# Input projection: a fifth column group in split precision, its low parts on GpSimd, and the S5 phase products on VectorE

## What is computed

```
h = rmsnorm(x) * w
a_v, a_g, b_u, c_z, c_xbc, c_dt = split(h @ w_in)      # w_in 2048 x 4112
ya = conformer_conv(a_v, a_g)                          # 31 taps, layernorm, silu
yb = s5(b_u)                                           # complex diagonal recurrence, 32 groups x 64 states
yc = mamba2(c_z, c_xbc, c_dt)                          # 4 taps, state-space product
x  = x + concat(ya, yb, yc) @ w_out
x  = x + cross_attention(rmsnorm(x), mem_k, mem_v)     # mem_k, mem_v = rmsnorm(mem) @ wk, @ wv
x  = x + conv_ffn(rmsnorm(x))
```

## Time and profile before

| | us |
|---|---|
| median of 3 runs | 1803.45 (1802.83 to 1803.63) |
| the profiled execution | 1805.04 |
| its span | 1803.3 |
| busy: TensorE, VectorE, ScalarE, GpSimd | 1784.9, 1139.3, 739.2, 258.9 |

### The profile page before, as it was taken

The page is one execution under the profiler, slowest core; times in us unless marked ns, Lnnn a source line. Parts: engine busy times, 40 slices in busy tenths (PEclk is TensorE's granted clock), DMA queues, the critical chain, the costliest instruction groups (busy, mean ns, idle before and its releaser), DMA issues.

```text
span 1803.3 us, 32857 instructions
## 1 busy us (share of the span) xinstructions
PE 1784.9 (99%) x12594; PEld 1640.2 (91%) x12594; DVE 1139.3 (63%) x1976; ACT 739.2 (41%) x1111; POOL 258.9 (14%) x273
## 2 busy tenths in 40 slices
PE   8999999999999999999999999999999999999998
PEld 7877898777779999866999999999999999999998
DVE  6999888888775564443456556665655566546444
ACT  3100575444453343342245344444433345444444
POOL 1024200133421310000132000000000000003200
PEclk9999999999999999999999999999999999999999
DMA  8333544556667585487555555555555556554552
GB/s 255 106 117 106 198 140 138 176 182 208 196 209 240 164 303 164 153 327 265 154 164 164 164 163 163 163 163 164 164 166 165 165 148 185 166 163 160 167 163 99
DMA packets 158390, 316.49 MB, mean 176 GB/s; under 512 B 16986, under 2 KB 39531, under 8 KB 153492
## 3 DMA queue, kind: packets, MB, share of 16 engines
q1 hardware_dynamic: 153525, 307.73, 54.5%
q10 hardware_dynamic: 4776, 7.56, 1.4%
HBM read 300.78 MB, written 14.89 MB: 175 GB/s over the span
## 4 chain that ended last, share of the span: by engine, by line
PE 93%; DVE 4%; DMA 2%; ACT 1%; issue 0%; ACTq 0%; SPq 0%; DVEq 0%
PE bank L909 22%; PE bank L911 21%; PE bank L910 21%; PE bank L872 20%; PE bank L1467 2%; PE bank L1479 1%; DVE xc L2638 1%; DMA kv<-in_cache_mem_v 1%; DMA xtok<-in_x_prompt 1%; PE bank L1489 1%; PE bank L1278 0%; DMA raw<-in_w_out 0%; DVE raw_lo L2665 0%; PE bank L1097 0%; PE bank L958 0%; PE bank L1312 0%
## 5 line engine op out<-in xcount | busy, mean ns | idle before, releaser
L909 PE MATMUL bank<-hhi,whi 128*128 128x288 f32 x2128 | 631.9, 297 | 0.9 <-DVE wlo L2918 0.9
L910 PE MATMUL bank<-hlo,whi 128*128 128x288 f32 x2128 | 628.5, 295 | 0.0
L911 PE MATMUL bank<-hhi,wlo 128*128 128x288 f32 x2128 | 626.3, 294 | 0.0
L2918 DVE TENSOR_TENSOR wlo<-raw,whi 128x1024 fp32r<-128x1024 f32 (+1 forms) x270 | 329.7, 1222 | 377.7 <-ACT whi L1950 377.1
L1950 ACT ACTIVATE whi<-raw 128x1024 fp32r<-128x1024 f32 (+1 forms) x270 | 283.2, 1049 | 509.8 <-PE bank L911 501.9
L911 PEld LDWEIGHTS bank<-hhi,wlo 128*128 128x128 f32 x2128 | 401.6, 189 | 0.0
L909 PEld LDWEIGHTS bank<-hhi,whi 128*128 128x128 f32 x2128 | 399.3, 188 | 2.3 <-DVE wlo L2918 1.9
L910 PEld LDWEIGHTS bank<-hlo,whi 128*128 128x128 f32 x2128 | 400.2, 188 | 0.1
L872 PE MATMUL bank<-hT,raw 128*128 128x288 f32 x640 | 160.1, 409 | 0.0
L872 PEld LDWEIGHTS bank<-hT,raw 128*128 128x128 f32 x640 | 120.0, 190 | 35.0 <-issue 3.1
L1877 ACT ACTIVATE khi<-raw 128x1024 fp32r<-128x1024 f32 x66 | 69.9, 1059 | 109.5 <-PE bank L872 106.4
(11 more groups left out here) (551 smaller groups left out, 2744.4 us busy)
## 6 DMA issues: line engine op xcount, KB each, us to landing
raw<-in_ffn_w_down SPq DMA_DIRECT2D x86, 512.0 KB, 3.8
raw<-in_ffn_w_gate SPq DMA_DIRECT2D x80, 512.0 KB, 3.7
raw<-in_ffn_w_up SPq DMA_DIRECT2D x80, 512.0 KB, 3.7
raw<-in_w_in SPq DMA_DIRECT2D x64, 512.0 KB, 3.7
raw<-in_xa_wk SPq DMA_DIRECT2D x32, 512.0 KB, 3.9
raw<-in_xa_wv SPq DMA_DIRECT2D x32, 512.0 KB, 4.2
raw<-in_w_out SPq DMA_DIRECT2D x32, 512.0 KB, 3.8
raw<-in_xa_wq SPq DMA_DIRECT2D x32, 512.0 KB, 4.0
```

What stands on the lines that cost most here:

```text
L909: pe.matmul(out, lhsT=wh[:, wo:wo + P], rhs=xh, start=first, stop=False)
L910: pe.matmul(out, lhsT=wh[:, wo:wo + P], rhs=xl, start=False, stop=False)
L911: return pe.matmul(out, lhsT=wl[:, wo:wo + P], rhs=xh, start=False, stop=last)
L2918: tt(wlo[:, s % 2, wsl], raw[:, s % 4, wsl], whi[:, s % 2, wsl].bitcast(F32), ALU.subtract)\
```

## The change

Five things change together:

- Slabs 32 to 39, the fifth group, become split slabs (`SPLIT_AT` 40 to 32).
- The low parts of slabs 32 to 47 are made by GpSimd (L783 of the changed kernel, semaphore `in_lo_g`), those of slabs 48 to 63 still by VectorE (`LOW_V`). The buffers stay as they were.
- The phase products go from GpSimd to VectorE: those of iteration j-1 stand between the turn of j and its adds. The turn back of j-1 goes ahead of the scans of j.
- TensorE feeds pairs 6 and 7 after slabs 33 and 36 (32 and 34 before), and takes the outputs of pairs 5, 6 and 7 after slabs 36, 39 and 42 (35, 37 and 39 before).
- ScalarE's list follows: `x_high` and the high parts of slabs 32 to 34 come ahead of the conformer's first taps, those of 35 to 41 before the loop over slabs 40 to 63. Four small additions of the conformer's input (`glu_a`) move from iterations 10 to 13 to iterations 6 to 9, and the last S5 output (`s5_y(3)`) from slab 41 to slab 43.

```diff
-        S5_IN = (17, 20, 22, 25, 27, 30, 32, 34)
+        S5_IN = (17, 20, 22, 25, 27, 30, 33, 36)
...
-        SPLIT_AT = 40
+        SPLIT_AT, LOW_V = 32, 48
+        S5_OUT = (22, 25, 27, 30, 32, 36, 39, 42)
...
-            for j in range(SJ):
-                pool.wait_ge(*at("s5_scanned", j + 1))
-                g_ = gri[:, j % 2, :, :]
-                if j >= 1:
-                    pool.wait_ge(*at("s5_h", 2 * j))
-                pool.tensor_tensor(hAB[:, 0, :, :], g_, tabC[:, j, :].unsqueeze(1).to_broadcast([P, 2, NP]),
-                                   ALU.mult).then_inc(S("s5_prod"), 1)
-                pool.tensor_tensor(hAB[:, 1, :, :], g_, tabS[:, j, :].unsqueeze(1).to_broadcast([P, 2, NP]),
-                                   ALU.mult).then_inc(S("s5_prod"), 1)
...
+            for x in range(SPLIT_AT, LOW_V):
+                pool.wait_ge(*at("kw_hi", x - SPLIT_AT + 1))
+                pool.tensor_tensor(raw_lo[:, x % 4, :], raw[:, x % 4, :], ihi_slot(x).bitcast(F32), ALU.subtract)\
+                    .then_inc(S("in_lo_g"), 1)
...
-                    if split:
-                        pe.wait_ge(*at("kw_lo", sl - SPLIT_AT + 1))
+                    if split and sl < LOW_V:
+                        pe.wait_ge(*at("in_lo_g", sl - SPLIT_AT + 1))
+                    if sl >= LOW_V:
+                        pe.wait_ge(*at("kw_lo", sl - LOW_V + 1))
...
-                    if x == S5_IN[pair] + 5:
+                    if x == S5_OUT[pair]:
                         s5_out(pair)
...
+            x_high(range(12))
+            in_split(32)
+            x_high(range(12, 14))
+            in_evac(3)
+            in_split(33)
+            x_high(range(14, KT))
+            in_split(34)
...
+            def s5_products(j):
+
+                v.wait_ge(*at("s5_scanned", j + 1))
+                g_ = gri[:, j % 2, :, :]
+                if j >= 1:
+                    v.wait_ge(*at("s5_h", 2 * j))
+                for i, tab in enumerate((tabC, tabS)):
+                    tt(hAB[:, i, :, :], g_, tab[:, j, :].unsqueeze(1).to_broadcast([P, 2, NP]), ALU.mult)\
+                        .then_inc(S("s5_prod"), 1)
...
+                if j >= 1:
+                    s5_products(j - 1)
...
-                me.sync()
+                gri_done = me.n
+                if j >= 1:
+                    s5_turn_back(j - 1)
+                me.reach(gri_done)
```

More of the change, by code:

```diff
@@ L65 @@
     "dve_norms": (("hmix", 16), ("hxa", 16), ("hffn", 16)),
-    "pool_setup": (("bsel", 2), ("s5_prod", 2 * SJ), ("s5_fin", 2), ("conf_sum", 2)),
+    "pool_setup": (("bsel", 2), ("s5_fin", 2), ("in_lo_g", 16), ("conf_sum", 2)),
     "pe_mixers": (("glu_mm", 4), ("ex_mm", 5), ("mem_t", 8), ("ps_t", 1),
@@ L1208, in kv_group @@
                     sl = NA + 8 * g + s
-                    pe.wait_ge(*at("kw_lo", N_SPLIT + 8 * g + s + 1))
+                    pe.wait_ge(*at("kw_lo", N_LOW_V + 8 * g + s + 1))
                     wh = khi[:, sl % 2, :].rearrange("p (k n) -> p k n", k=2)
@@ L1767, in _, with x_high, in_split @@
             in_evac(2)
+            def x_high(tiles):
+                for k in tiles:
+                    wait_used_A(sc_, 24 + k // 2)
+                    sc_.wait_ge(*at("x_lo", k + 1))
+                    a(xhi[:, k, :], hT[:, k, :], ACT.Copy).then_inc(S("x_hi"), 1)
+            def in_split(x):
+                wait_raw(sc_, x // 4, x % 4)
+                if x >= SPLIT_AT + 2:
+                    wait_used_A(sc_, x - 2)
+                if x == 48:
+                    sc_.wait_ge(*at("s5_prod", 2 * SJ))
+                    sc_.wait_ge(*at("s5_turned", 2 * SJ))
+                a(ihi_slot(x), raw[:, x % 4, :], ACT.Copy).then_inc(S("kw_hi"), 1)
+            x_high(range(12))
+            in_split(32)
+            x_high(range(12, 14))
             in_evac(3)
+            in_split(33)
+            x_high(range(14, KT))
+            in_split(34)
             def first_tap(dst, dst_s, src, src_s, w, b, name):
@@ L1790, in gelu @@
                     a(uT[:, t, :], uT[:, t, :], ACT.Gelu_apprx_tanh).then_inc(S("s5_gelu"), 1)
[L1792 to L1807, removed]
             def mem_square(t):
@@ L1815, in mem_square @@
                   accum_out=msum[:, t:t + 1]).then_inc(S("mem_sq"), 1)
-            x_high(range(12))
-            in_split(SPLIT_AT)
-            x_high(range(12, 14))
+            for x in range(35, 41):
+                in_split(x)
             in_evac(4)
-            in_split(SPLIT_AT + 1)
-            x_high(range(14, KT))
+            in_split(41)
             def mem_rows(t, c0, c1):
@@ L1877, in k_split @@
                 a(khi[:, y % 2, :], raw[:, y % 4, :], ACT.Copy).then_inc(S("kw_hi" if y < NKV else "w_hi"), 1)
-            for x in range(SPLIT_AT, NA):
+            for x in range(40, NA):
                 if x == NA - 1:
@@ L1882, in _ @@
                     k_split(0)
-                elif x > SPLIT_AT:
+                elif x > 40:
                     in_split(x + 1)
@@ L2543, in last_state, with in_split @@
                     me.step(v.tensor_copy(fin[:, i, j:j + 1], hri[:, j % 2, i, NP - 1:NP]))
+            def in_split(x):
+                v.wait_ge(*at("kw_hi", x - SPLIT_AT + 1))
+                tt(raw_lo[:, x % 4, :], raw[:, x % 4, :], ihi_slot(x).bitcast(F32), ALU.subtract)\
+                    .then_inc(S("kw_lo"), 1)
             for j in range(SJ):
@@ L2563, in _ @@
                     .then_inc(S("s5_scanned"), 1)
-                if j in (10, 11, 12, 13):
-                    glu_a((j - 10,))
+                if j in (6, 7, 8, 9):
+                    glu_a((j - 6,))
                 if 2 <= j < 10:
                     x_low((6 + j,))
-                if j >= 1:
-                    s5_turn_back(j - 1)
                 if j == 8:
@@ L2573, in _ @@
                     s5_y(1)
+            s5_products(SJ - 1)
             s5_turn_back(SJ - 1)
@@ L2644, in conv_c @@
                         q.then_inc(S("conv_c_taps"), 1)
-            def in_split(x):
-                v.wait_ge(*at("kw_hi", x - SPLIT_AT + 1))
-                tt(raw_lo[:, x % 4, :], raw[:, x % 4, :], ihi_slot(x).bitcast(F32), ALU.subtract)\
-                    .then_inc(S("kw_lo"), 1)
-            in_split(SPLIT_AT)
-            in_split(SPLIT_AT + 1)
             def mem_lo(k):
@@ L2672, in _ @@
                        60: (14, 16), 61: (17, 17)}
-            for x in range(SPLIT_AT, NA):
+            for x in range(40, NA):
                 if x == NA - 1:
                     k_split(0)
-                elif x > SPLIT_AT:
+                elif x >= LOW_V - 1:
                     in_split(x + 1)
@@ L2679, in _ @@
                     s5_y(2)
+                if x == 43:
                     s5_y(3)
```

1 line of the change is left out of this document (added).

## The result

The changed kernel takes 1823.31 us at the median of four runs (1822.35 to 1824.58) against 1803.54 for the kernel before: 1.0103 of it, 95% interval 1.0090 to 1.0116. It is 19.8 us slower. (The ratios here and in the table are those on record. They are not the quotients of the two medians, from which they differ by some 0.002 at most; here that quotient is 1.0110.) I had forecast slower, 1811.5, and a range that ended at 1819. The profiled execution took 1822.77 us, its span is 1821.1, 17.8 longer than before's.

The account below looks back on a forecast made before the run. TensorE, busy 99% of the span, was taken to bound the kernel. Profiled 1805.0 plus 8.0 (slab 43 +6.2, slabs 44 to 47 +1.5 and +0.3) gave 1813.0, less 1.6 for the median: 1811.5 us; range 1799 to 1819.

Parts of the forecast that it names:

- step 5: SyncE's queue: glu_w and raw slab 43 wait for the last product; slab 43 starts 11.5 us after it, +6.2.
- step 6: Slabs 44 to 47: turns through ScalarE and GpSimd of 3.56 us against 3.19, +1.5, and lengthening by taps, +0.3.
- Step 4: Recurrence: each GpSimd low part of 2.2 us costs VectorE 1.65; last product at about 213, 8.5 us later.
- rival C: Recurrence: scans held too or GpSimd starved, 2.35 us per part; last product at 220, 1818.5 us; chance 0.20 with D.
- rival D: Products on VectorE are dear, waiting for GpSimd's parts; shows as long L2540; C's time, 1818.5; chance 0.20 with C.
- Step 1: Slabs 32 to 39 become split on TensorE, 3.19 instead of 3.88 us each, saving 5.5 us while fed.
- Step 2: Recurrence's earliest end by TensorE's feeding: last product at 203.8 us, now about 204.5, so nothing gained or lost.
- Step 3: VectorE's recurrence loop: moving products there costs nothing, a 1.08 us stall exchanged for 1.2 of work; iteration 5.2 us.
- The check on VectorE's side: Loop 8.5 later, five low parts add 8.2, eight parts removed give -9.1: +7.6 us, about TensorE's +8.0.
- Rival A: Recurrence: low parts hide in turns, scans and waits; last product at 203.8, slab 43 earlier, 1798 to 1800.5 us; chance 0.17.
- From slab 48 on nothing differs: From slab 48 to the end, the accumulated lateness stays unchanged.

Follow-up runs that it names:

- e7: Changed kernel with each low part on GpSimd replaced by two memsets of the same tile, correction left out; 1803.20 us, 0.9996 of the kernel before.
- e5: Changed kernel with 24 unused matmuls on TensorE filling the stop ahead of slab 43; 1820.27 us, 1.0112 of the kernel before.
- e11: Changed kernel with GpSimd's low parts replaced by two memsets and SyncE's product wait and glu_w load behind raw slab 44; 1799.67 us, 0.9967 of the kernel before.
- e3: Kernel before with only the phase products moved to VectorE and the turn back ahead of the scans; 1805.69 us, 1.0006 of the kernel before.
- e6: Changed kernel with every GpSimd low part cut to its first 512 columns, used for both slab halves; 1803.83 us, 1.0000 of the kernel before.
- e4: Kernel before with only the low parts of slabs 40 to 47 moved to GpSimd; 1808.96 us, 1.0022 of the kernel before.
- e1: Changed kernel with SyncE's last-product wait, glu_w load and two mtok loads moved behind raw slabs 46 and 47; 1819.61 us, 1.0070 of the kernel before.

## Why the prediction was wrong

The direction held, and so did the chain of causes: low parts hold VectorE, the last product is late, SyncE's queue passes it on, slab 43 stops. The sizes failed in two steps: the last product came 7.0 us later than forecast, step 5 took 0.6 less, and step 6 took 3.4 more. That is 9.8, the whole of 17.8 less 8.0.

**Step 4, the price of a part, was the one that failed.** I put it at three quarters of 2.2, 1.65 us, and took off 2.5 for parts that fall into waits: last product at 213. Measured: 1.97 a part, 19.7 for ten; with 199.0 that is 218.7, and it came at 220.0. I left it open whether a scan is held, and priced a part from a row that had only an add beside it; the rows of after and e7 show that scans are held while GpSimd reads, and not while it only writes. A part was also longer than 2.2 us, 2.35 at least. And the 2.5 had nothing to be taken from: a loop that is late has no waits left, and VectorE was busy 56.00 of 56. This is rival C's working (220 for the last product, 231.5 for slab 43; measured 220.0 and 230.9), to which, together with rival D, I gave 0.20. Its price of the whole 2.35 was too high for a part, and the deduction of 2.5 made up for that, so that C's number was met by luck. D's sign, long L2540, is there too, four of the eleven held instructions and 6.4 of the 21.5 us. They are held by the same parts as the adds and scans. No run has the parts with the products left on GpSimd in the recurrence, so D's share stays open.

**Step 6 was too small by 3.4.** I gave slabs 43 to 47 1.8 us; they took 21.1 us (230.94 to 252.0) where before took 15.9, +5.2. Some 2.5 of it is the granted clock after the stop, as e5 shows (18.6 us for the same slabs, +2.7): a term that the prediction did not have. Most of the rest are stops of 1.67 ahead of slab 45, whose part took 3.44 us, and 0.63 ahead of slab 47. The turn alone, which I had at 1.5, costs 0.9 in e11, where GpSimd's two memsets take 1.97 us (16.8 us for the five slabs).

**Step 1 was right** within what the runs tell: 5.5 us forecast, and e11 gave 5.6 by the medians, 4.0 by the spans, 4.4 at the start of slab 43 (213.93). **Step 2's** floor of 203.8 was 205.3 with nothing held (e7). **Step 3 was right**: the products cost nothing clear of noise by themselves (e3), and an iteration of the change without a part takes 5.05 us (195.60 to 200.65), where I had 5.2. **Step 5 was right** to within 0.6: 11.5 us from the last product to slab 43 forecast, 10.9 measured. Its pieces were off in opposite ways: the slab landed in 6.6 us, not 7.5, and its low part took 2.59, not 2.2. What it missed is that a stop costs more than its length.

**The check on VectorE's side** reached the same +8 only because it used the same 1.65; with the measured lateness of 15.5 us and 1.97 a part it gives +16.3. It was no independent check either: it took VectorE to be the bound behind the recurrence, and there VectorE waits, in its timeline for slab 48's high part:

```profile
249.27 1.23 DVE L2562 TENSOR_TENSOR raw_lo<-raw,ihi 128x1024 fp32r<-128x1024 f32 x1 [10.13 <-ACT ihi L1782]
```

"From slab 48 on nothing differs" held: the spans differ by just what slab 48 starts later.

**Rival A** was to be told by a last product before 206.8. e7 reached 205.3, and slab 43 started at 215.56, A's 215.3. Yet slab 48 came only 1.9 us earlier than before and the ratio shows no gain; it takes e11's order too.

**The range** ended at C's time, 1819, and C had no clock in it: with the +5.2 of step 6 in place of 1.8 it gives 1822.

## What to carry to other kernels

Before work goes to an idle GpSimd, look at what VectorE runs at that time. In these traces adds, products, scans and taps with two operands in SBUF stood while GpSimd read, or GpSimd's part stood for them: a part that takes 2.4 us on GpSimd cost VectorE 1.97 where making it itself costs 1.14. A part cost VectorE nothing where it lay beside turns that read PSUM (two parts of e6), and a deduction for hiding in waits holds only as long as the loop is not late. Then look at the moved work's own path: behind the recurrence the slabs waited for the part itself (e4). Where an in-order queue holds a load behind a late event, price the stop with the clock that follows it.

## What was not expected of the hardware

- A scan of 128x256 with its decay and data in SBUF took 2.76 to 2.86 us beside a GpSimd subtraction, 0.68 beside a GpSimd memset of like length.
- The one that is held is not always VectorE: beside products of 128x960 (1.91 and 1.92 us) a GpSimd part took 4.26 and 4.59 us (e1) where it takes 2.35.
- After a stop of 6.8 us TensorE's granted clock was 0.50 from 230 to 236 us while it worked without a pause; with the stop filled by idle matmuls it was 1.00 throughout (e5).
